# ScalarE converts the embedding gate's third weight block before it evicts the embedding's fourth product

## The reference

```python
    for i in range(DEPTH):                        # DEPTH = 1
        ...                                       # mixing, then h = h + rmsnorm(mix)
        u = rmsnorm(h, ffn_pre_norm[i])
        gate, up = jnp.split(u @ w_gate_up[i], [D_FF], axis=-1)
        y = (jax.nn.silu(gate) * up) @ w_down[i]
        h = h + rmsnorm(y, ffn_post_norm[i])
        h = h + (p[i] @ ple_proj[i]) * jax.nn.sigmoid(h @ ple_gate[i])
    return h                                      # and on into second_block
```

## Time and profile before

| | us |
|---|---|
| median of 3 runs | 994.4 |
| lowest and highest of them | 994.0, 994.59 |
| the profiled execution's own time | 989.33 |
| its span in the trace | 987.6 |
| TensorE busy in it | 796.2 (81%) |
| mean granted clock | 0.932 of full |

### The profile page before, as it was taken

One profiled execution on the slowest core, in us unless ns is written; L12 is line 12 of the kernel. 1 busy time (PEld: TensorE's weight loads), 2 busy tenths in 40 slices (PEclk: granted clock), 3 DMA queues, 4 the chain that ended last, 5 costly groups with the idle time before them and its releaser, 6 DMA issues.

```text
span 987.6 us, 21230 instructions
## 1 busy us (share of the span) xinstructions
PE 796.2 (81%) x8283; PEld 655.7 (66%) x8284; DVE 486.1 (49%) x794; ACT 355.9 (36%) x488; POOL 51.5 (5%) x145
## 2 busy tenths in 40 slices
PE   5999889699999998879999998885575575685473
PEld 5999579699999998768989864543232332353241
DVE  3645687767787855375797543331221211331222
ACT  5432486364555644163885231110101101110102
POOL 4000100000000000001040000000000000000000
PEclk9999999899999999798999999998887988998877
DMA  7586322269898755343328767999999999999994
GB/s 269 178 281 241 110 84 88 86 250 339 294 313 294 261 187 185 103 152 106 109 69 330 288 257 285 422 429 425 424 430 425 423 430 426 423 430 425 424 428 167
DMA packets 89011, 278.77 MB, mean 282 GB/s; under 512 B 8031, under 2 KB 67850, under 8 KB 71562
## 3 DMA queue, kind: packets, MB, share of 16 engines
q1 hardware_dynamic: 88270, 276.86, 72.5%
q10 hardware_dynamic: 700, 1.36, 0.4%
HBM read 277.15 MB, written 1.05 MB: 282 GB/s over the span
## 4 chain that ended last, share of the span: by engine, by line
PE 54%; DMA 29%; DVE 9%; ACT 5%; issue 2%; SPq 0%; DVEq 0%; ACTq 0%
DMA projR<-in_w_up 20%; PE bank L385 10%; PE bank L387 9%; PE bank L386 9%; PE bank L1935 8%; DMA Whi<-in_w_up 7%; PE bank L1958 2%; DVE Whi_r L323 2%; PE acc L1632 1%; PE acc L1630 1%; PE acc L1627 1%; PE bank L1632 1%; PE bank L1630 1%; PE bank L1627 1%; ACT Whi_r L314 1%
## 5 line engine op out<-in xcount | busy, mean ns | idle before, releaser
L385 PE MATMUL bank<-R_r,Whi_r 128*128 128x256 f32 x800 | 234.7, 293 | 19.0 <-DVE R_r L2214 4.9
L386 PE MATMUL bank<-R_r,Whi_r 128*128 128x256 f32 x800 | 231.1, 289 | 0.0
L387 PE MATMUL bank<-R_r,Whi_r 128*128 128x256 f32 x720 | 207.1, 288 | 0.0
L385 PEld LDWEIGHTS bank<-R_r,Whi_r 128*128 128x128 f32 x800 | 158.4, 198 | 24.1 <-issue 13.7
L386 PEld LDWEIGHTS bank<-R_r,Whi_r 128*128 128x128 f32 x800 | 158.9, 199 | 0.1
L387 PEld LDWEIGHTS bank<-R_r,Whi_r 128*128 128x128 f32 x720 | 141.9, 197 | 0.0
L2717 DVE TENSOR_TENSOR V<-V,bank 64x256 f32<-64x256 f32 x34 | 14.4, 424 | 233.6 <-ACT V L1393 233.6
L1393 ACT ACTIVATE V<-bank 64x256 f32<-64x256 f32 x34 | 12.8, 376 | 217.6 <-PE bank L1935 217.6
L1935 PE MATMUL bank<-Whi,S 128*32 128x256 f32 x832 | 59.3, 448 | 37.1 <-DMA Whi<-in_w_up 32.3
L323 DVE TENSOR_TENSOR Whi_r<-Wlo,Whi_r 128x1024 fp32r<-128x1024 f32 x54 | 64.9, 1246 | 46.6 <-ACT Whi_r L314 46.5
L2159 DVE TENSOR_TENSOR Whi_r<-Wlo,Whi_r 128x2048 fp32r<-128x2048 f32 x33 | 75.6, 2289 | 24.7 <-ACT Whi_r L1179 11.7
(11 more groups left out here) (494 smaller groups left out, 1551.4 us busy)
## 6 DMA issues: line engine op xcount, KB each, us to landing
Wlo<-in_w_in SPq DMA_DIRECT2D x24, 1024.0 KB, 5.2
Wlo<-in_w_gate_up SPq DMA_DIRECT2D x22, 1024.0 KB, 5.1
Whi<-in_w_gate SPq DMA_DIRECT2D x10, 2048.0 KB, 31.1
Whi<-in_w_up SPq DMA_DIRECT2D x10, 2048.0 KB, 35.6
Whi<-in_w_down SPq DMA_DIRECT2D x10, 2048.0 KB, 37.3
Wlo<-in_w_gate SPq DMA_DIRECT2D x9, 2048.0 KB, 32.8
projR<-in_w_up SPq DMA_DIRECT2D x9, 2048.0 KB, 37.7
Wlo<-in_w_up SPq DMA_DIRECT2D x9, 2048.0 KB, 37.2
```

Source lines behind the costliest of these rows:

```text
L385: pe.matmul(o, w_hi[:, c], tile(x_hi, k), start=(k == 0), stop=False)
L386: pe.matmul(o, w_hi[:, c], tile(x_lo, k), start=False, stop=False)
L387: mm = pe.matmul(o, w_lo[:, c], tile(x_hi, k), start=False, stop=(k == KT - 1))
```

## The change

In ScalarE's queue the copy of the embedding's fourth product, `pp_out(3)`, and the wait ahead of it move from in front of block (1,0) of the gate to behind it. Nothing else is changed; two lines go and three come, so lines after L1215 count three higher.

```diff
@@ -1202,7 +1202,7 @@
             act_token_root(act, "nfpost", token_rms("nfpost"))
 
             act_source(act, "pgate", hT, SRC_LO, lambda b: act.wait_ge(*upto("h2_ready", b + 1)))
-            for b in range(1, 4):
+            for b in range(1, 3):
                 act.wait_ge(*upto("pp_done", b))
                 pp_out(b)
 
@@ -1214,6 +1214,9 @@
                 act.wait_ge(*upto(f"pgate_done{j}", 1))
                 act_hi(act, pgate, 1, j)
                 gate_out(0, j)
+                if j == 0:
+                    act.wait_ge(*upto("pp_done", 3))
+                    pp_out(3)
             act_hi(act, proj2, 0, 0)
             act.wait_ge(*upto("pgate_done0", 2))
             gate_out(1, 0)
```

## The result

| us | before | after |
|---|---|---|
| median of 8 runs each | 992.22 | 985.73 |
| lowest and highest | 990.01, 994.59 | 982.31, 987.1 |
| the profiled execution's own time | 989.33 | 984.35 |

The ratio is 0.9933 with a 95% interval of 0.9913 to 0.9953: the change takes 6.5 us off (forecast: 6.28). The time itself lies under the range that I gave (986.4 to 991.0), because the kernel before, too, is 992.2 over eight runs and not the 994.4 of its first three.

What follows compares the result with a forecast made beforehand. TensorE waits ahead of gate block (1,0) because ScalarE's wait for the fourth product's copy stands before work needed next. Wait 4.93 plus clock 1.35 gives 6.28 us; 994.4 - 6.28 = 988.1 us, range 986.4 to 991.0.

Steps and rivals of the forecast that it cites:

- The wait: Ahead of gate block (1,0): TensorE starts it at 418.45 instead of 423.38, 4.93 us earlier.
- The clock: Gate blocks (1,0) and (1,1): the low clock stretch from 424.16 goes with the idle time, worth 1.35 us.
- What is late next: Block (1,1): the moved copy now stands ahead of its rounding, but inputs are ready with 1.63 us of cover.
- Whether it reaches the end: Behind the gate: busy TensorE passes the shift on, expert transfers start 6.28 us earlier, so the full gain reaches the end.
- the prediction's own last sign of being wrong: At the end: first expert load comes 6.3 us earlier, but the span is not shorter by as much.
- the clock gives part back: Rival: pauses before the 445.1 stretch meet the throttle differently; one more low stretch costs 2.6 us, giving 990.7; chance 8%.
- The low stretch at 445.1: Behind the gate: 6.4 us at low clock after shorter pauses, kept in the sum before and after alike.
- against the median, 994.4 - 6.28 = 988.1: Whole kernel: the gain subtracted from the median of the runs shown, giving 988.1 us, -0.63%.
- The range that I derived: Whole kernel: 986.9 to 989.3 us, from the clock term's bounds and the runs' spread.
- The 2.0 us that I took as the bound of a measurement: Whole kernel: 0.2% (2.0 us) is what a measurement can tell from no change, since runs lie within 0.6 us.

Runs made afterwards that it cites:

- e1_half: Kernel before, with the fourth product's copy moved only behind the rounding of block (1,0), still ahead of table load and eviction; ratio 0.9968 against before, -3.2 us.
- e4_fill: Kernel before, with 36 matmuls of no use on TensorE behind the fourth product; ratio 0.9985 against before, -1.5 us.
- c4_before: Kernel before, unchanged, in one more profile (the fourth of four later ones); 990.31 us.
- c1_before: Kernel before, unchanged, in one more profile (the first of four later ones); 991.33 us.
- a1_after: Changed kernel, run again without further change; median 986.07 us beside 992.71, ratio 0.9931; its profiled execution took 986.12 us.
- c3_before: Kernel before, unchanged, in one more profile (the third of four later ones); 994.98 us.
- e3_slack: Changed kernel, with six more ScalarE copies behind the moved copy, delaying the rounding of block (1,1); ratio 0.9993 against before, median 991.36 us.

## Why the prediction was right, and where it was wrong

- **The wait, 4.93 us**: right. Block (1,0) starts 1.54 us behind the fourth product instead of 6.47. Its inputs were ready 2.7 us earlier (eviction over at 418.40, needed at 421.09). e1_half puts the wait on the eviction.
- **The clock, 1.35 us**: right in size; e4_fill, which fills the pause and leaves the wait, measures 1.48 (1.35 against c4_before). The forecast's 1.35 already had the slower first matmul of block (1,0) in it, 0.12 us the other way. Sum in the gate 6.28, measured 6.28 in the first profile, 6.29 in the second.
- **What is late next**: right. Block (1,1) does not wait, its cover is 1.57 us (predicted 1.63), and a later place for the copy brings nothing.
- **Whether it reaches the end**: right in size, 6.5 and 6.6 us in two sets of runs, though with intervals 4 and 5 us wide it is in part luck that they come that close. The profiles that show it best are c4_before and c1_before beside after: product at 419.6 to 419.9, 87 us behind the gate and 51.8 to the load of R in all three, and the times differ by 5.96 and 6.98. Other pairs differ by other amounts. The pair with an early product (before and a1_after) differs by 3.2 us, because a1_after lost 3.0 us behind its first expert load (54.81). That is the prediction's own last sign of being wrong: the first expert load is 6.5 us earlier and the span only 3.2 shorter. The pair with a late product (c3_before and after) differs by 10.6, because there the kernel before lost the 3.0 us, and 1.75 behind the gate. Since c3_before has the same 54.80 without the change, the loss is not the change's doing. Whether the change makes it more frequent (the rival "the clock gives part back") can't be told from two profiles of the changed kernel; the runs as a whole show the full amount, within their intervals. The low stretch at 445.1, which I left in the sum on both sides, was shorter in the first profile of after (0.73 over 6 us).
- **The level, which is what failed.** The step that was wrong is "against the median, 994.4 - 6.28 = 988.1" and the sentence behind it, that runs of before lie within 0.6 us. With eight runs the median is 992.22, which gives 985.9 by the same subtraction; measured 985.73. 50 runs of before in three sets reach from 989.25 to 995.75: 29 at or under 991.4, 17 from 993.59 up, 4 between. The three first ones all lay in the upper group, and the profiled execution's own time, 989.33, 5.07 us under them, stood beside the sum: it was evidence that the kernel also has executions 4 to 5 us lower. I noted the difference and left it out of the range. A range of 983 (989.33 - 6.28) to 989 or 990 would have carried what the rows said. (The range that I derived had a slip besides: with the clock term at 0 its upper end is 989.5, not 989.3.) The 2.0 us that I took as the bound of a measurement is, for the same reason, too small for a few runs: e3_slack's interval is 4.3 us wide.

What stays open: why the clock falls between 60 and 140 us in some executions of an unchanged program and not in others, and why the low stretches behind the gate and ahead of the load of R are long in some and short in others. The runs show that it does and what it costs, not what decides it.

## What to carry to other kernels

In an engine's queue, a wait for something that nobody needs soon costs what stands behind it; look for idle time whose releaser is a product with a late reader, and move that product's copy behind the work that the bounding engine wants next. Work out the cover that is left for the next wait, since that tells whether the place is good, or only better. Predict the difference from distances within one trace, and set the level by all that is known of it: where the profiled execution's own time and the median differ by more than the runs do, the kernel has more than one level, and the range must hold both.

## What the runs showed of the hardware

- One unchanged program on one core has times from 989.25 to 995.75 us, most of the difference from where TensorE's clock falls to 1.2 GHz: up to 3.0 us ahead of the fourth product, 1.6 to 2.1 behind the gate, 3.0 ahead of the load of R, each there in some executions and not in others. A few runs can all come from one of the levels.
- Low stretches cost what the matmuls lose in pitch, 0.213 us instead of 0.12 (1.46 of 3.34 us), where TensorE is the bound. Where VectorE's tiles are, a low stretch of 3.4 us cost nothing (14.78 us with it and without).
- A pause of 4.58 us on TensorE brought a low stretch of 3.34 us behind it in the first profile of before and one like it in four later ones; with matmuls of no use in the pause it did not come. The length of the pause alone doesn't tell: 2.69 us (e1_half) brought none in the gate, 2.25 (e3_slack) brought one of 3.4.
- A Copy behind a Sigmoid needed no table load, and the Sigmoid behind it needed none again: the table load at 416.51 is the only one in the gate. It took 1.28 us, and the next instruction started 1.29 us after the load's start.
